# Orders in four stages of a two-layer kernel: token sums in groups, high parts first, a gate quarter split around the state products, the last chunk's norm order, and q before the last v panel

## The reference

```python
# block 1
h = rms_norm(x, g) * (1 + sc1) + sh1          # the modulation comes from c @ ada_w
y = hybrid_mixer(h)                           # forgetting attention beside a 31-tap convolution
x = x + g1 * rms_norm(y, post_g)              # "post norm"
h = rms_norm(x, g) * (1 + sc2) + sh2          # "pre norm"
x = x + g2 * rms_norm(swiglu_ffn(h), post_g)
# block 2, layer A: state space in chunks of 128 tokens, 4 groups of 8 heads
z, xbc, dt = split(h @ in_w);  xbc = silu(conv4(xbc))
for each chunk:
    scores = (C @ B.T) * exp(cum_t - cum_s), causal
    y = scores @ (x * dt) + (C @ state) * exp(cum)
    state = state * exp(cum_end) + B.T @ (x * dt * exp(cum_end - cum))
y = (y + D * x) * silu(z);  y = rms_norm per group * norm_g;  x = x + gate * (y @ out_w)
# layer B: stick-breaking attention, 16 heads, blocks of 128 queries
k, v = split(modulate(x) @ kv_w);  q, z = split(modulate2(x) @ in_w)
a = exp(log_sigmoid(l) + sum of log_sigmoid(-l) over the later keys), l = q @ k.T / 8
x = x + gate * ((a @ v) * silu(z) @ out_w);  return rms_norm(x) * final_g
```

## Time and profile before

| | |
|---|---|
| median of 3 runs | 1438.09 us (1435.17 to 1441.22) |
| profiled execution | 1437.19 us |
| its span, first to last instruction | 1435.4 us, mean granted TensorE clock 0.97 |
| TensorE busy | 1360.9 us, 95% of the span |
| VectorE, ScalarE, GpSimd busy | 57%, 41%, 28% |
| DMA | 181 MB, mean 126 GB/s |

### The profile page before, as it was taken

How to read it: one execution, slowest core, us unless ns; L and a number is a source line. 1 busy time by engine, 2 the same in 40 slices (tenths; PEclk the granted TensorE clock), 3 DMA queues, 4 the chain that set the end, 5 groups by cost and what they waited for, 6 DMA issues and landing times. The chain is left out here.

```text
span 1435.4 us, 19530 instructions
## 1 busy us (share of the span) xinstructions
PE 1360.9 (95%) x7904; PEld 1078.1 (75%) x7904; DVE 823.6 (57%) x965; ACT 588.3 (41%) x848; POOL 405.6 (28%) x191
## 2 busy tenths in 40 slices
PE   5999999889999999999999999988998999999996
PEld 3777867668888888887788876766776898777774
DVE  3789853476655544333757556677733822466544
ACT  4323656333222222112444456776522422455451
POOL 0000000039987887998100000000000050233310
PEclk9999999989999999999799999999999999999998
DMA  9433061215454455553222243333122432110121
GB/s 384 160 134 132 30 235 63 84 34 210 177 194 180 171 218 191 190 191 147 92 89 88 96 126 89 118 118 133 59 102 86 151 132 89 59 60 30 59 89 59
DMA packets 41350, 181.12 MB, mean 126 GB/s; under 512 B 3392, under 2 KB 20160, under 8 KB 21312
## 3 DMA queue, kind: packets, MB, share of 16 engines
q1 hardware_dynamic: 40128, 171.73, 33.2%
q10 hardware_dynamic: 1152, 8.39, 1.7%
HBM read 173.75 MB, written 6.36 MB: 125 GB/s over the span
## 5 line engine op out<-in xcount | busy, mean ns | idle before, releaser
L193 DVE TENSOR_TENSOR wlo<-raw,whi 128x2048 fp32r<-128x2048 f32 x95 | 260.8, 2745 | 183.1 <-ACT whi L189 180.6
L200 POOL TENSOR_TENSOR ada_raw<-ada_raw,cs 128x2048 f32<-128x2048 f32 x36 | 142.0, 3944 | 509.6 <-DVE h2lo L451 458.6
L271 PE MATMUL ps<-hhi,whi 128*128 128x512 f32 x640 | 252.0, 394 | 2.4 <-PEq L562 0.8
L271 PE MATMUL ps<-hhi,wlo 128*128 128x512 f32 x640 | 249.4, 390 | 0.0
L271 PE MATMUL ps<-hlo,whi 128*128 128x512 f32 x640 | 249.1, 389 | 0.0
L189 ACT ACTIVATE whi<-raw 128x2048 fp32r<-128x2048 f32 x95 | 181.5, 1911 | 143.6 <-PE ps L1309 91.3
L209 POOL TENSOR_TENSOR ada_raw<-ada_raw 128x1024 f32<-128x1024 f32 x72 | 169.4, 2353 | 5.6
L271 PEld LDWEIGHTS ps<-hhi,whi 128*128 128x128 f32 x640 | 120.2, 188 | 28.6 <-issue 2.4
L271 PEld LDWEIGHTS ps<-hhi,wlo 128*128 128x128 f32 x640 | 120.1, 188 | 25.7
L271 PEld LDWEIGHTS ps<-hlo,whi 128*128 128x128 f32 x640 | 120.3, 188 | 24.3
L2036 POOL TENSOR_TENSOR x<-x,rest 128x256 f32<-128x256 f32 (+3 forms) x32 | 49.0, 1532 | 163.7 <-DVE rest L2331 163.7
(11 more groups left out here) (373 smaller groups left out, 2806.4 us busy)
## 6 DMA issues: line engine op xcount, KB each, us to landing
raw<-panels SPq DMA_DIRECT2D x87, 1024.0 KB, 4.9
ada_raw<-ada SPq DMA_DIRECT2D x48, 1024.0 KB, 6.7
first<-ada SPq DMA_DIRECT2D x8, 1024.0 KB, 19.6
bc<-ac_rows SPq DMA_DIRECT2D x32, 256.0 KB, 3.7
raw<-panels ACTq DMA_DIRECT2D x8, 1024.0 KB, 5.1
x_kept<-x SPq DMA_DIRECT2D x2, 2048.0 KB, 9.6
x<-x_kept SPq DMA_DIRECT2D x2, 2048.0 KB, 8.2
x<-x_in SPq DMA_DIRECT2D x1, 2048.0 KB, 9.3
```

Of the source, the lines that this page charges most:

```text
L193: e.tensor_tensor(wlo[:, c % 2, :, :], raw[:, c % 2, :, :], whi[:, c % 2, :, :].bitcast(F32), ALU.subtract).then_inc(lo_split, 1)
L200: e.tensor_tensor(ada_raw[:, c % 2, :, :], ada_raw[:, c % 2, :, :], cs[:, which, :].unsqueeze(2).to_broadcast([P, KT, 256]), ALU.mult).the ...
L271: mm = e.matmul(ps[:, 2 * (qc % 2) + b, :], w[:, c % 2, 2 * k + b, :], src[part][:, k, :], **flags)
```

## The change

- In both post-norms and in the final norm, the sums of squares stand in groups after banks 3, 5 and 7 (`SUMS_AFTER`).
- In the pre-norm products TensorE takes for each tile the four matmuls with the high part of the activation first, waiting for it alone, and the two with the low part behind a wait of their own. Two coefficient instructions on VectorE move ahead.
- In the state space, at the end of chunks 0 to 2, one gate quarter is cut in half: six matmuls stay before the third state product, six go behind the fourth.
- In the last chunk: ScalarE issues the transfer of one panel behind the squares of group 1, not in the loop; VectorE's split of a weight panel, the norm of group 0 and the reciprocal of group 1 stand behind the reciprocal of group 0, before the gate product of group 2.
- In the last stage the q panel comes eighth and the last v panel ninth; the first projection, not the first logits, waits for the ninth's copy; the split of panel 10 moves behind the first Sigmoids and scan; a Sigmoid of one column stands after the eighth panel's split.

```diff
@@ -299,6 +299,7 @@
 ORDER = [7, 6, 0, 1, 2, 3, 4, 5]
+SUMS_AFTER = {3: (0, 1, 2), 5: (3, 4), 7: (5, 6)}
 SPARE = {1: 0, 3: 1, 5: 3, 7: 5}
@@ -351,11 +352,10 @@
     part(b).then_inc(N["bank_done"] if j < KT - 1 else panels_used, 1)
-    if j == 2:
+    if j == 3:
         pe.wait_ge(*no("kept", 1))
-        token_sums(pe, no, 0, 0, sq, ORDER[0])
-    if j >= 2:
-        token_sums(pe, no, 0, j - 1, sq, ORDER[0])
+    for t in SUMS_AFTER.get(j, ()):
+        token_sums(pe, no, 0, t, sq, ORDER[0])
 token_sums(pe, no, 0, KT - 1, sq, ORDER[0])
@@ -471,12 +471,13 @@
 for k in range(k0, k1):
-    pe.wait_ge(*no("lo_ready", k + 1))
-    for b in range(2):
-        for n, (w, part) in enumerate(PASSES):
-            mm = pe.matmul(ps[:, 2 * (qc % 2) + b, :], w[:, c % 2, 2 * k + b, :],
-                           (thi, tlo)[part][:, k, :], start=(k == 0 and n == 0),
-                           stop=(k == KT - 1 and n == 2), skip_group_check=True)
+    for part, weights in ((0, (whi, wlo)), (1, (whi,))):
+        pe.wait_ge(*no("lo_ready" if part else "hi_ready", k + 1))
+        for b in range(2):
+            for w in weights:
+                mm = pe.matmul(ps[:, 2 * (qc % 2) + b, :], w[:, c % 2, 2 * k + b, :],
+                               (thi, tlo)[part][:, k, :], start=(k == 0 and part == 0 and w is whi),
+                               stop=(k == KT - 1 and part == 1), skip_group_check=True)
 if k1 == KT:
@@ -1196,8 +1197,8 @@
 dve.sem_inc(pair_free[1], 2)
+pre1["coefs"](dve)
 post1["dve"](dve)
-pre1["coefs"](dve)
 pre1["dve"](dve)
@@ -1285,9 +1286,9 @@
 post2["coefs"](dve)
+pre2["coefs"](dve)
 stream(dve, "ffn_out", lo=True, keep_last=2)
 post2["dve"](dve)
-pre2["coefs"](dve)
 pre2["dve"](dve)
@@ -1488,19 +1489,19 @@
 
-def z_quarter(k):
+def z_quarter(k, k2=(0, 4)):
 
...
     cp, qp = c0 + p, q0 + p
-    if k % 4 == 0:
+    if k % 4 == 0 and k2[0] == 0:
         pe.wait_ge(lo_split, cp + 1)
         pe.wait_ge(pair_free[qp % 2], qp // 2 + 1)
-    for kt in range(k0, k0 + 4):
+    for kt in range(k0 + k2[0], k0 + k2[1]):
         for j, (wt, part) in enumerate(PASSES):
...
                            stop=(kt == KT - 1 and j == 2))
-    if k % 4 == 3:
+    if k % 4 == 3 and k2[1] == 4:
         mm.then_inc(panels_used, 1)
@@ -1592,13 +1593,13 @@
     if g == 2:
-        for k in LAYING_OUT[c + 1][0:1]:
-            z_quarter(k)
+        z_quarter(LAYING_OUT[c + 1][0], (0, 2))
     if g >= 2:
...
               stop=True).then_inc(M["st"], 1)
+z_quarter(LAYING_OUT[c + 1][0], (2, 4))
 
@@ -1746,7 +1747,7 @@
     taken += 1
-for p in taken_at(n - 5) if n >= 5 else ():
+for p in taken_at(n - 5) if 5 <= n < NN - 3 else ():
     load_panel(act, c0 + p + 4, 0)
@@ -1757,6 +1758,8 @@
 group_squares(1)
+for p in taken_at(NN - NB):
+    load_panel(act, c0 + p + 4, 0)
 hi_part(act, 0)
@@ -1889,9 +1892,6 @@
             split_lo(dve, c0 + p + 2, 0)
-if c == TB - 1 and g == MG - 1:
-    norm_lo(dve, 0)
-    group_rs(dve, 1)
 dve.wait_ge(M["yd"], 2 * gi + 2)
@@ -1909,6 +1909,11 @@
     group_rs(dve, 0)
+    for n in range(c * NB, NN - 3):
+        for p in taken_at(n):
+            split_lo(dve, c0 + p + 2, 0)
+    norm_lo(dve, 0)
+    group_rs(dve, 1)
 if g == MG - 1:
@@ -1918,10 +1923,6 @@
         gate_part(dve, g)
-        if g == 1:
-            for n in range(c * NB, NN - 3):
-                for p in taken_at(n):
-                    split_lo(dve, c0 + p + 2, 0)
 if c < TB - 1:
@@ -1993,6 +1994,8 @@
 
+if j in (7, 8):
+    return c0 + 15 - j
 if j < 9 or j >= 16:
@@ -2040,9 +2043,9 @@
 for j in range(1, 9):
-    if j == 8:
+    if j == 7:
         pre4["all_low"](pe)
-    in_panel(pe, c0 + j, q0 + j, 0, (h2hi, h2lo) if j == 8 else (hhi, hlo), 4 <= j < 8)
+    in_panel(pe, c0 + j, q0 + j, 0, (h2hi, h2lo) if j == 7 else (hhi, hlo), j in (4, 5, 6, 8))
     if j == 6:
@@ -2052,7 +2055,6 @@
 if n == 0:
-    pe.wait_ge(pair_free[0], (q0 + 8) // 2 + 2)
     pe.wait_ge(pair_free[1], (q0 + 7) // 2 + 2)
@@ -2101,6 +2103,8 @@
     pe.wait_ge(lo_split, c + 1)
+if mh == 0:
+    pe.wait_ge(pair_free[0], (q0 + 8) // 2 + 2)
 if mh >= 2:
@@ -2184,12 +2188,9 @@
     mm.then_inc(nsem["bank_done"] if j < KT - 1 else panels_used, 1)
-    if j == 2:
-        token_sums(pe, fin, 0, 0, fsq, ORDER[0])
-    if j >= 3:
-        token_sums(pe, fin, 0, j - 2, fsq, ORDER[0])
-for j in range(KT - 2, KT):
-    token_sums(pe, fin, 0, j, fsq, ORDER[0])
+    for t in SUMS_AFTER.get(j, ()):
+        token_sums(pe, fin, 0, t, fsq, ORDER[0])
+token_sums(pe, fin, 0, KT - 1, fsq, ORDER[0])
 spread(pe, fin, 0, ORDER[0])
@@ -2199,8 +2200,8 @@
 bank = ps[:, 2 * pair:2 * pair + 2, :]
-if 4 <= j < 8:
-    r = j - 4
+if j in (4, 5, 6, 8):
+    r = min(j - 4, 3)
     act.activation(v2[:, :, r * 256:(r + 1) * 256],
@@ -2208,7 +2209,10 @@
     act.activation(qhi[:, 0:2, :], bank, ACT.Copy, scale=scale).then_inc(B["qhi"], 1)
-split_hi(act, c0 + j + 2, 0)
+if j < 8:
+    split_hi(act, c0 + j + 2, 0)
+if j == 7:
+    act.activation(warm[:, 7:8], ones[:, 0:1], ACT.Sigmoid)
 if j < 2:
@@ -2250,6 +2254,8 @@
                    scale=-1.0).then_inc(B["keep"], 1)
+if n == 0:
+    split_hi(act, c0 + 10, 0)
 if 2 <= n <= NU + 1:
@@ -2281,12 +2287,13 @@
                       ALU.subtract).then_inc(pair_free[pair], 1)
-elif j == 8:
+elif j == 7:
     dve.wait_ge(B["qhi"], 1)
...
                              op1=ALU.subtract).then_inc(pair_free[pair], 1)
-split_lo(dve, c0 + j + 2, 0)
+if j < 8:
+    split_lo(dve, c0 + j + 2, 0)
 if j < 2:
@@ -2331,6 +2338,8 @@
     scan.then_inc(B["rest"], 1)
+if n == 0:
+    split_lo(dve, c0 + 10, 0)
 if n >= STEPS and n % STEPS == 0 and n // STEPS <= HALVES:
```

## The result

The changed kernel takes 1421.8 us (median of 4 executions, 1420.92 to 1422.05) against 1438.68 us before (4 executions, 1435.17 to 1441.22): ratio 0.9883, interval 0.9862 to 0.9905. Forecast were 1422.5 us in a range of 1416.5 to 1430, faster with 0.88. So the change is worth 13 to 17 us, and a difference of 1 to 3 us between two kernels is not to be read from their medians. In this document such differences come from the traces: the duration of one stage between two fixed instructions, which repeats to 0.1 us in most stages. One execution, of run i1, took 1750.13 us at a mean granted clock of 0.71 and is left out of every comparison.

The account below looks back on a forecast made before the run. TensorE, busy 1360.9 of 1435.4 us, was taken as the bound. Gains of 3.8 + 2.2 + 2.2 + 3.5 + 3.8 = 15.5 off 1437.2, plus 0.9 for the median, gave 1422.5 us, range 1416.5 to 1430.

Parts of the forecast that it names:

- token sums: Two post-norms and final norm: two groups of row sums between banks instead of five save TensorE 3.8 us.
- high part first, coefficients: Pre-norm products: TensorE starts at the first high part, coefficients come earlier; 2.2 us, bounds 0 and 2.4.
- half quarter: Ends of three chunks: six gate matmuls hide the 0.79 us wait before the transposes; 2.2 us, bounds -1.1 and +2.4.
- last chunk: Transfer, split, mask and norm orders of the last chunk: 3.5 us, bounds -2.2 to +5.3.
- last stage: q panel before the last v panel: 2.5 us of wait plus 1.3 of clock, 3.8 us; bounds 1.0 and 4.0.
- VectorE could set the pace: Lower case for the token sums: if VectorE set the pace there, the gain would be 0.
- The ring: Last chunk: engines wait on each other, ScalarE's decays 6.09 us late behind a transfer; opening it brings the first norm 5.3 us earlier.
- the wait of 1.09: Last chunk, before the second norm: forecast to go, since TensorE's spread is in time; 1.1 us gained.
- the one of 2.09: Last chunk, wait before the last gate product: forecast to stay, because it hangs on ScalarE behind the high parts.
- the gate product's delay: Last chunk: the gate product now follows the first norm, giving back 2.2 us; alone it sets the lower bound, -2.2.
- Signs named: Profile signs: grouped sums, earlier first products, no idle before transposes, prompt decays, 3 to 4.5 us pause before fourth squares, prompt logits.
- (d): Rival: pause before the fourth squares drops the clock lastingly, 0.2 us more per matmul, ending about 1445 to 1450; chance 0.04.

Follow-up runs that it names:

- i1: Changed kernel with the third output panel's high and low parts and the fourth squares ahead of the third norm's work, fourth spread later: 1424.5 us, ratio 0.9917.
- e1: Changed kernel with the token sums alone put back to a group behind each bank, in all three norms: 1427.63 us, ratio 0.9941.
- e3: Changed kernel with the gate quarter whole again ahead of the third state product: 1425.71 us, ratio 0.9918.
- e6: Changed kernel with only VectorE's order of the last chunk put back; ScalarE's transfer stays behind the second group's squares: 1421.67 us, ratio 0.9893.
- e5: Changed kernel with the last stage's panels in the order of before, q behind the last v panel: 1425.9 us, ratio 0.9924.

## Why the prediction held

The time was right to 0.7 us by the first measurement, to 2.1 by the second. Step by step, forecast and measured:

| part | forecast | measured by stages |
| --- | --- | --- |
| token sums | 1.35 + 1.35 + 1.14 = 3.8 | 1.30 + 1.25 + 1.07 = 3.6 |
| high part first, coefficients | 1.06 + 0.33 + 0.85 = 2.2 | starts earlier by 1.0, 0.46 and 0.8; 2.0 arrives by means, 1.5 like with like; the two old traces taken singly give 1.1 and 2.8 |
| half quarter | 3 x 0.74 = 2.2 | 0.83 + 0.95 + 0.97 = 2.75, less 1.63 where the clock falls (1.1 in the profiled execution) |
| last chunk | 3.5 | 3.3 (two kernels against six) |
| last stage | 3.8 | 3.5 |
| sum | 15.5 | 15.2 with the clock held in chunk 2, 14.7 with 1.5 in the second row |

The profiled executions differ by 15.4, but that so near a number comes out is in part luck: 1.63 of the gain went in a clock fall, and 1.7 came from an earlier start that the change has no part in.

**Sums.** The size of an alternation, put together from the earlier trace rows as 0.15 and 0.23, was right: three fewer and the moved sum give 1.30 for 1.35. That VectorE could set the pace is excluded by e1.

**Quarter.** The prediction charged each place 0.05 to 0.1 for the additional switches. By the starts in e3 and in the changed kernel this cost was too small, and so was the gain beside it: the additional switches cost 0.43, and the pause to be filled is 1.35, since the 0.79 counts from the modelled end of products that the next group's start overlaps by 0.57. The two errors went opposite ways, and that 0.74 came near the 0.83 to 0.97 measured was luck. What the prediction left out is that this stretch holds two waits of about 1 us that it doesn't touch, behind which the clock may fall. In the profiled execution it fell, and 1.63 of the 2.75 went in it.

**The ring.** The time line worked out in advance held link by link: the first norm 5.1 us earlier (forecast 5.3; by shifts, 1000.38 to 988.98, less the 6.3 already there), output products 6.5 earlier (6.5), the wait of 1.09 gone, the one of 2.09 kept, a pause of 2.92 in exchange (3 to 4.5). Its slow restart is mostly hidden as forecast: in e6, with the clock kept, TensorE comes early to the third panel and waits 0.76 for the split instead. But the part's cause was drawn too wide. By e6 the transfer alone gives 4.5 us, and VectorE's half of the edit takes 0.95 to 1.2 of them back, through the gate product that now stands behind the norm ("the gate product's delay").

**Last stage.** The wait of 2.37 became one of 0.29, the first twelve projection matmuls take 3.04 for 4.07, and the logits ahead of them 0.4 less: 3.5 (forecast 2.5 of wait and 1.3 of clock); the moved split and the second scan brought no new wait.

**Signs named.** All came: sums in two groups, first products at the first high part, no idle before transposes, decays without a long wait, the pause (2.92, just under the 3 to 4.5 named), and logits right behind the last panel. One sum among the rivals doesn't fit: in (d) 192 matmuls at 0.2 us more are 38 us, which ends at about 1461 and not at 1445 to 1450; nothing of that kind came. What was not forecast is the clock in chunk 2. The profiled executions also differ by about 1.7 us before the first edit counts (ScalarE's first squares, which wait for x, start at 9.73 for 10.97 us, and waits for transfers in the attention stage); by the other traces, which by 45 us into the span are 0.7 to 2.8 us later than this one with the same code up to there, that is no effect of the change.

## What to carry to other kernels

A pause of TensorE behind an edit is not the price of the edit but the next thing to edit: the removed ring left 2.92 us of waiting, whose own cause (splits and squares behind high parts in ScalarE's queue, with ScalarE idle for 3.09 and 5.76 us before those high parts) was worth another 6 us. Move all links of such a chain together, since i1 moved two of three and won nothing in its stage, and the same VectorE order was a loss with the pause and a gain without. Differences of a few us are read from stage durations over several traces, not from medians, and not from one trace.

## What the hardware showed

- The same code behind the same two waits (0.88 and 1.02 us) ran on at full clock in 8 of 10 traces, and fell to the lower level in 2 (the changed kernel's first, e6), for 1.63 us. At the first pre-norm the way from the first product to the next stage takes 13.2 to 14.7 us, in two clusters.
- A wait costs more than itself: 3.50 us in i1 brought 2.5 at the lower clock behind it, 2.37 in e5 1.4 (4.41 us for the first twelve projection matmuls, 3.04 in the changed kernel), while behind 0.78 at the end of chunk 1 in e3 the granted clock stayed at 1.00.
- A wait of TensorE in a row is counted from the modelled end of the matmuls before it: 0.78 us in e3 where 1.35 could be filled.
- Between products of 512 columns and short groups of sums each alternation costs about 0.36 us beside the sums' own time (1.30 less 0.21 for the moved sum, over three), and between gate products and state products 0.43.
- ScalarE's next instruction starts 1.29 to 1.30 us after a table load of 1.28 begins (995.56 and 996.85 before, 983.04 and 984.34 after).
